# Second attention of a two-block transformer: ScalarE's order in odd works, earlier loads and values' copy, four projection chunks among the last works

## What is computed

```python
def swa_sink_mixer(h, w_in, w_out, sinks, cos, sin):      # 16 query heads, 2 key/value heads, head size 64
    q, k, v = jnp.split(h @ w_in, [qd, qd + kd], axis=-1)
    q, k = apply_rope(q), apply_rope(k)
    o = banded_attention(q, k, v, 128, sinks)             # causal, window 128
    return o @ w_out

# banded_attention, for each block of 128 queries and its 256 keys
s = q @ k.T * scale, masked to -inf outside the window
m = max(max(s), sink); e = exp(s - m)
p = e / (sum(e) + exp(sink - m));  o = p @ v
```

## Time and profile before

| | us |
|---|---|
| median of three runs (lowest, highest) | 2071.42 (2065.5, 2071.64) |
| profiled execution, its own time | 2069.99 |
| its span in the trace | 2068.2 |
| TensorE (PE) busy, share of the span | 1969.9 (95%) |
| DVE, POOL, ACT busy | 1114.8, 943.0, 695.6 |
| main part of the second attention, from `score(2)` to the output projection | 844.9 to 915.75 |

### The profile page before, as it was taken

How to read it: one execution, slowest core, us unless ns; L and a number is a source line. 1 busy time by engine, 2 the same in 40 slices (tenths; PEclk the granted TensorE clock), 3 DMA queues, 4 the chain that set the end, 5 groups by cost and what they waited for, 6 DMA issues and landing times.

```text
span 2068.2 us, 26747 instructions
## 1 busy us (share of the span) xinstructions
PE 1969.9 (95%) x10152; PEld 1616.7 (78%) x10152; DVE 1114.8 (54%) x1729; ACT 695.6 (34%) x1217; POOL 943.0 (46%) x552
## 2 busy tenths in 40 slices
PE   6999999999999999788999999999999999999997
PEld 5888776788888877667888888788897778888886
DVE  7576776864554667656422313676463338345163
ACT  3353564432222233544322213342343333222122
POOL 1465554465444445444444444543363335444442
PEclk9999999999999999999999999999999999999999
DMA  7775332455556415522333222222242123223231
GB/s 286 239 217 163 108 98 81 164 183 183 190 176 203 154 52 177 150 71 72 101 94 96 97 93 101 72 68 76 100 137 90 62 71 109 95 93 101 92 102 61
DMA packets 79986, 252.18 MB, mean 122 GB/s; under 512 B 12160, under 2 KB 12672, under 8 KB 79616
## 3 DMA queue, kind: packets, MB, share of 16 engines
q1 hardware_dynamic: 79872, 250.61, 37.3%
HBM read 235.21 MB, written 15.37 MB: 121 GB/s over the span
## 4 chain that ended last, share of the span: by engine, by line
PE 71%; issue 12%; POOL 7%; DVE 6%; ACT 3%; DMA 1%; SPq 0%; POOLq 0%; DVEq 0%; ACTq 0%
PE ps L901 19%; PE ps L903 19%; PE ps L902 19%; POOL wl L793 5%; PE ps L1150 2%; PE ps L1090 2%; PE ps L1122 2%; ACT pr L2556 1%; PE ps L1416 1%; DVE st L1859 1%; POOL al L849 1%; PE ps L1441 1%; PE ps L969 1%; POOL x L841 1%; PE ps L964 1%
## 5 line engine op out<-in xcount | busy, mean ns | idle before, releaser
L793 POOL TENSOR_TENSOR wl<-raw,wh 128x1024 fp32r<-128x1024 f32 x309 | 770.2, 2498 | 966.8 <-ACT wh L2411 966.7
L2411 ACT CAST wh<-raw 128x1024 fp32r<-128x1024 f32 x309 | 322.3, 1050 | 931.3 <-PE ps L903 854.7
L901 PE MATMUL ps<-ah,wh 128*128 128x512 f32 x1240 | 488.6, 394 | 1.5 <-DVE pair L1791 1.5
L902 PE MATMUL ps<-ah,wl 128*128 128x512 f32 x1240 | 483.4, 390 | 0.0
L903 PE MATMUL ps<-al,wh 128*128 128x512 f32 x1240 | 483.3, 390 | 0.0
L901 PEld LDWEIGHTS ps<-ah,wh 128*128 128x128 f32 x1240 | 233.2, 188 | 53.2 <-issue 3.0
L901 PE MATMUL ps<-hh,wh 128*128 128x512 f32 x688 | 271.0, 394 | 1.8 <-DVE hl L2368 1.7
L902 PEld LDWEIGHTS ps<-ah,wl 128*128 128x128 f32 x1240 | 233.3, 188 | 49.3 <-issue 1.5
L903 PEld LDWEIGHTS ps<-al,wh 128*128 128x128 f32 x1240 | 233.2, 188 | 49.2
L903 PE MATMUL ps<-hl,wh 128*128 128x512 f32 x688 | 269.9, 392 | 0.0
L902 PE MATMUL ps<-hh,wl 128*128 128x512 f32 x688 | 268.1, 390 | 0.0
(11 more groups left out here) (373 smaller groups left out, 2806.8 us busy)
## 6 DMA issues: line engine op xcount, KB each, us to landing
raw<-in_units SPq DMA_DIRECT2D x309, 512.0 KB, 3.5
ada_mlp<-in_ada SPq DMA_DIRECT2D x64, 512.0 KB, 3.4
ada<-in_ada SPq DMA_DIRECT2D x16, 512.0 KB, 16.0
qs<-qscr SPq DMA_DIRECT2D x32, 256.0 KB, 3.7
ada_in<-in_ada SPq DMA_DIRECT2D x16, 512.0 KB, 3.6
ks<-kscr SPq DMA_DIRECT2D x24, 256.0 KB, 4.6
x<-in_xT SPq DMA_DIRECT2D x1, 2048.0 KB, 13.1
qscr<-rot_h SPq DMA_DIRECT2D x16, 128.0 KB, 2.4
```

The source lines that it names most:

```text
L793: nc.gpsimd.tensor_tensor(wl[:, slot], raw[:, slot], wh[:, slot].bitcast(F32), ALU.subtract).then_inc(lo_done, 1)
L901: nc.tensor.matmul(out_ap, wh[:, slot, k], high[:, k0 + k], start=first and k == 0, stop=False)
L902: nc.tensor.matmul(out_ap, wl[:, slot, k], high[:, k0 + k], start=False, stop=False)
L2411: a.copy(wh[:, slot], raw[:, slot]).then_inc(hi_done, 1)
```

## The change

The diff has seven parts. On SP, the keys and the first two queries of group 1 are loaded ahead of the store of rotary result 10, behind two waits (result 8 stored, works 0 and 1 scored). On POOL, the last two low parts ahead of the attention wait until all 11 rotary results are made. On PE, one more unit runs ahead of the early scores (5 and 2 instead of 4 and 3 units around them). On DVE, the copy of v out of its bank (line 2124) runs between the last rotary's sums and its low part instead of behind that low part; the early attention stays behind the third query pair. On ACT, `copy(t-2)` runs ahead of `exponentials(t)` in odd steps. On PE, the first four chunks of the first unit of `swa_out` (12 matmuls) run in steps 17 and 18, two chunks ahead of `turn(15)` and two ahead of the last value; the first waits until the last work's exponentials have read the bank. `gemm_squared` then runs that unit's chunks 4 to 7 and the other seven units.

```diff
--- before.py
+++ after.py
@@ -641,10 +641,10 @@
                     sp.dma_start(qscr[4 * grp + j, 64 * low_part:64 * low_part + 64].rearrange("(a r) t -> r a t", a=2),
                                  rot[32 * j:32 * j + 32].bitcast(F32)).then_inc(rot_kept[index % 2], 16)
 
-        def loads_during(plan):
+        def loads_during(plan, first=0):
 
             for w, (g, kind, j) in enumerate(plan.works):
-                if g + 1 < GROUPS:
+                if w >= first and g + 1 < GROUPS:
                     sp.wait_ge(sc_made, plan.scored[w][-1])
                     if not plan.nsa:
                         if j == 0:
@@ -773,8 +773,13 @@
         store_q(8, 1)
         units(u + 14, u + 15)
         store_q(9, 2)
+        sp.wait_ge(rot_kept[0], rot_count(8))
+        sp.wait_ge(sc_made, PLAN_SWA.scored[EARLY - 1][-1])
+        load_k(PLAN_SWA, 1, 0)
+        for j in range(EARLY):
+            load_q(PLAN_SWA, 1, j)
         store_q(10, 3)
-        loads_during(PLAN_SWA)
+        loads_during(PLAN_SWA, EARLY)
         units(FIRST["swa_out"] + RING, FIRST["mix_out"] + 6)
         sp.wait_ge(pooled, 4)
         sp.dma_start(me[:], src["memT"]).then_inc(x_in, 16)
@@ -871,6 +876,7 @@
         added_norm(1, "swa_in")
         over_units(pool, FIRST["swa_in"] + RING, FIRST["swa_in"] + RING + 9, low)
         attention(PLAN_SWA, early=True)
+        pool.wait_ge(rot_made, 11)
         over_units(pool, FIRST["swa_in"] + RING + 9, FIRST["swa_out"] + RING, low)
         attention(PLAN_SWA)
         over_units(pool, FIRST["swa_out"] + RING, FIRST["mlp1"] + RING, low)
@@ -1009,10 +1015,26 @@
             for c in range(DC):
                 square_sum(c)
 
-        def gemm_squared(first, high, low, ready=None, ks=DC, adds=False, between=None):
-
-
-            for c in range(DC):
+        def chunks(u, k0, k1, high, low, ready):
+
+            n, slot = done[0], u % RING
+            if k0 == 0:
+                bank_free(n)
+                pe.wait_ge(lo_done, u + 1)
+            for k in range(k0, k1):
+                pe.wait_ge(ready[0], ready[1] + k + 1)
+                nc.tensor.matmul(ps[:, n % RING], wh[:, slot, k], high[:, k], start=k == 0, stop=False)
+                nc.tensor.matmul(ps[:, n % RING], wl[:, slot, k], high[:, k], start=False, stop=False)
+                mm = nc.tensor.matmul(ps[:, n % RING], wh[:, slot, k], low[:, k], start=False, stop=k == DC - 1)
+            if k1 == DC:
+                mm.then_inc(unit_used, 1)
+                done[0] += 1
+
+        def gemm_squared(first, high, low, ready=None, ks=DC, adds=False, between=None, made=0):
+
+            if made:
+                chunks(first, made, DC, high, low, ready)
+            for c in range(1 if made else 0, DC):
                 gemm(first + c, 1, high, low, ready=ready, ks=ks)
                 if between:
                     between(c)
@@ -1044,7 +1066,7 @@
                                       small("ones")[:, 0:1], start=True, stop=True)
             mm.then_inc(ada_sum, 1)
 
-        def attention(plan, early=None):
+        def attention(plan, early=None, fill=None):
 
             if not early:
                 pe.wait_ge(evac, done[0] if plan.nsa else done[0] - 1)
@@ -1158,6 +1180,11 @@
                     score(w)
                 return
             for t in range(0 if plan.nsa else EARLY, len(works) + LAG + 1):
+                if t == len(works) + 1 and fill:
+                    pe.wait_ge(p_made, plan.expd[-1][-2])
+                    fill(0, 2)
+                if t == len(works) + 2 and fill:
+                    fill(2, 4)
                 if t == EARLY + 1 and not plan.nsa:
                     pe.wait_ge(v_placed, 1)
                 if t < len(works):
@@ -1297,12 +1324,12 @@
         gemm_first(FIRST["swa_in"], ah, al, "swa_in")
         gemm(FIRST["swa_in"] + 3, 1, ah, al)
         ada_turn(7)
-        gemm(FIRST["swa_in"] + 4, 4, ah, al)
+        gemm(FIRST["swa_in"] + 4, 5, ah, al)
         attention(PLAN_SWA, early=True)
-        gemm(FIRST["swa_in"] + 8, UNITS_SWA_IN - 8, ah, al)
+        gemm(FIRST["swa_in"] + 9, UNITS_SWA_IN - 9, ah, al)
         assert done[0] % RING == 3
-        attention(PLAN_SWA)
-        gemm_squared(FIRST["swa_out"], ah, al, ready=(o_split, 2 * GROUPS), adds=True)
+        attention(PLAN_SWA, fill=lambda k0, k1: chunks(FIRST["swa_out"], k0, k1, ah, al, (o_split, 2 * GROUPS)))
+        gemm_squared(FIRST["swa_out"], ah, al, ready=(o_split, 2 * GROUPS), adds=True, made=4)
         mlp("mlp1", 32)
 
         u = FIRST["mix_in"]
@@ -1776,7 +1803,7 @@
 
         rots = [0]
 
-        def rotary(to, whole=False, query=False):
+        def rotary(to, whole=False, query=False, between=None):
 
             n = banks[0]
             a, b = ps[:, n % RING], ps[:, (n + 1) % RING]
@@ -1794,6 +1821,8 @@
             v.tensor_tensor(to[:, 2], to[:, 2], to[:, 3], ALU.add).then_inc(kc_made if whole else rot_sum, 1)
             if whole:
                 return
+            if between:
+                between()
             rotary_low(to, query)
 
         def rotary_low(to, query):
@@ -2117,11 +2146,10 @@
         rotary(pair_s)
         ada_take(7)
         ada_coef(1, 5)
-        for p in range(4):
+        for p in range(3):
             rotary(pair_s, query=True)
-            if p == 2:
-                attention(PLAN_SWA, early=True)
-        v.tensor_copy(v_t[:], bank()).then_inc(evac, 1)
+        attention(PLAN_SWA, early=True)
+        rotary(pair_s, query=True, between=lambda: v.tensor_copy(v_t[:], bank()).then_inc(evac, 1))
         attention(PLAN_SWA)
         copy_out(coef_at(1, 2))
         norm_shared("mlp1", coef_at(1, 3), coef_at(1, 4), factor=coef_at(1, 2))
@@ -2584,9 +2612,12 @@
                     exponentials(w)
                 return
             for t in range(0 if plan.nsa else EARLY, len(works) + LAG + 2):
+                copy_first = not plan.nsa and t % 2 == 1
+                if copy_first and t < len(works) + LAG:
+                    copy(t - LAG)
                 if t < len(works):
                     exponentials(t)
-                if LAG <= t < len(works) + LAG:
+                if not copy_first and LAG <= t < len(works) + LAG:
                     copy(t - LAG)
                 for unit in plan.after.get(t - LAG - 1, ()):
                     if plan.is_last(unit):
```

## The result

| | before | after |
|---|---|---|
| median of four runs each, us | 2070.68 | 2052.52 (2051.55 to 2054.64) |
| profiled execution, its own time | 2069.99 | 2054.64 |
| its span | 2068.2 | 2052.8 |

The ratio of the runs is 0.9919, interval 0.9900 to 0.9937: 0.8% faster. The medians differ by 18.2 us; the forecast had said 17.75 less than the profiled execution, 2052.2. Single runs of one kernel on one chip spread over 1.5 to 9 us, and what a part is worth is read more sharply inside the attention, between two instructions of one trace. Even there the stretches up to `score(5)` can differ by 3.3 us between two executions of the same instructions, as the last run shows.

The account below looks back on a forecast made before the run. PE, busy for 95% of the span, was taken to bound the kernel. -2.05 - 5.0 - 6.7 - 4.0 = -17.75 against the profiled 2069.99 gave 2052.2 us, range 2047 to 2061.

Parts of the forecast that it names:

- Part 1: Unit ahead of the early scores: group 0's queries land under it, PE reaches `score(2)` sooner by that wait, -2.05 us.
- Part 2: `score(2)` to `score(3)`: v copied earlier, low part without POOL's tensor_tensors, but POOL's lock moves to line 1867; 0 us.
- Part 3: `score(3)` to `score(5)`: group 1's loads moved ahead, 12.73 us becomes 7.7; -5.0 us.
- a rival had with 0.25 and 1.7 us: PE's new stop before `score(3)` is followed once by 1.2 GHz, costing up to 1.7 us: 2053.9; chance 0.25.
- the forecast's own case: Whole kernel: the parts sum to -17.75 us, 2052.2; chance 0.42.
- Part 4: Steady pairs: ACT's copy ahead in odd steps, 7.81 us a pair becomes 6.55, bound by ACT and DVE; -6.7 us.
- the rival in which it holds them back: Odd steps on ACT: the copy ahead delays the exponentials, pairs stay at 7.81, 2058.9; chance 0.07.
- Part 5: `score(15)` to the projection: waits on ACT's and DVE's copies and lost clock shrink, chunks fill the time; -4.0 us.
- The slower rival: Attention: the clock stays at 1.2 GHz throughout, a pair takes 12.6 us instead of 7.81, 2092; chance 0.02.

Follow-up runs that it names:

- the last run: Only ACT's order of the change (copies ahead of the exponentials in odd steps), on the kernel before; 2062.44 us, ratio 0.9967.
- the three further edits together: On the changed kernel: POOL's tensor_tensors behind the works, the last low part behind the values' copy, ACT's high part ahead of odd exponentials; 2049.06 us, ratio 0.9905.

## Why the prediction held, point by point

*Part 1* was right: the unit covers the queries' landing. It gave 0.27 us more than the wait in brackets; the trace of the copies alone (42.73 with a wait of 1.42) says the same, so a stop cost PE some 0.25 us beyond what its row shows.

*Part 2* came out at its price, 0, and with the mechanism named, the lock on line 1867. One sub-step was wrong: it said that POOL is released by the new wait at 845.3. POOL was still in the scales of works 0 and 1; its tensor_tensor began behind them at 846.58, which is 845.59 on the axis of before, and without the wait nothing changes. That the scales ended so near the forecast release, and the lock with them (847.95 on that axis, forecast 848.2), was luck. Nor is it the wait that frees the low part here: it runs beside the scales instead of the tensor_tensors, as in every trace with the unit ahead of the early scores, and in that of the copies alone; in the run without the unit the wait did hold POOL. The price 0 is luck in part, too: before, the low part's 3.08 us came from the same kind of meeting, which the trace of the copies alone shows missed by the same instructions, with 4.46 us for this stretch. Against that trace parts 1 to 3 give 2.76 us, not 6.03. Of the change's seven parts, POOL's wait and v's copy are worth nothing in the changed kernel, each undone by itself.

*Part 3* was mis-sized, -3.69 for -5.0. The stop of 3.25 us brought the half clock that a rival had with 0.25 and 1.7 us: the stretch takes 9.04 us against 7.37 in the kernel with the tensor_tensors late, which has the full clock there, 1.67 less, and against 7.79 in the run without the chunks, where the half clock was shorter by half. So on the trace the rival came true, and the forecast's own case, with no half clock, did not; that the median lies at 2052.5 and not at the rival's 2053.9 is within what single runs spread. That the median came within 0.3 us of the forecast is luck: the parts, in the traces, miss its sum by 1.5.

*Part 4* was right in its mechanism and 0.1 us off per pair. The loop of ACT and DVE is 6.65, not 6.55: line 1896 now falls on a multiplication of POOL's in every odd step from 5 on (0.48 for 0.23, so 0.25 more up to ACT's start), while DVE's factor and maxima took 0.13 less than their terms in the sum (0.29 and 1.36, counted from start to start, for 0.38 and 1.40). PE's own pair was put too high, at 6.32 for 6.15 or less, since the pair less its wait keeps what a stop costs beyond its row, as in part 1; the first pair ran at PE's pace, as said. The loop's rows in after, DVE's, POOL's, then ACT's:

```profile
872.79 0.16 DVE L1915 TENSOR_TENSOR st<-st 128x4 f32<-128x4 f32 x1 [0.82 <-ACT st L2587]
...
873.08 1.25 DVE L1888 TENSOR_REDUCE st<-ps 128x1 f32<-128x256 f32 x4
...
874.44 0.48 DVE L1896 TENSOR_SCALAR st<-st,neg_sinks 128x4 f32<-128x4 f32 x1
```

```profile
873.26 2.06 POOL L819 TENSOR_SCALAR pr<-pr,st,sm 128x256 f32<-128x256 f32 x4 [0.33 <-DVE st L1916]
```

```profile
873.82 0.48 ACT L2603 COPY pt<-ps 128x384 f32<-128x384 f32 x1 [0.70 <-PE ps L1144]
...
875.01 0.48 ACT L2584 ACTIVATE pr<-ps,st 128x256 f32<-128x256 f32 x1 [0.71 <-DVE st L1896]
...
876.90 0.59 ACT L2608 CAST ah<-ps 128x512 fp32r<-128x512 f32 x1
877.37 0.51 ACT L2584 ACTIVATE pr<-ps,st 128x256 f32<-128x256 f32 x1
```

The copy is done at 874.3, 0.7 us before the odd exponentials are released, so the rival in which it holds them back is out. That the loop binds was shown by the run that took its `high` out of it.

*Part 5* was right: -3.82. The chunks give 2.38 of it. The copies exchange the wait of 2.8 for waits on POOL and DVE, and what they give by themselves is the clock: 1.44 where it holds (13.06 before, 11.62 without the chunks), 0.02 where it fell again (13.04, the copies alone). Undoing the copies costs the end 2.87, and that trace has the half clock there, too.

The slower rival did not come: at 96% busy the steady part kept the full clock.

## What to carry to other kernels

When a wait on PE's path is taken away, work out the loop that binds next; here the place of one copy on ScalarE decided 1.2 us of every 7.8. A wait or a move that a trace seems to ask for may be void once another part of the same change has shifted the neighbours: undo each by itself. A collision between two engines that one trace shows may be missing from the next execution of the same instructions: before a part is priced by it, look at a second trace. And work that has time, such as GpSimd's tensor_tensors here, was better placed behind the dense chain of small VectorE operations than beside it: moving two of them gave 3.3 us more in the trace, and the three further edits together 5.2 (92.72 against 97.91; 2049.06 against 2053.55 by the medians of the same chip).

## What the runs showed of the hardware that was not expected

- A 128 x 4 tensor_scalar on DVE, 0.23 us by itself, took 1.88 beside a GpSimd tensor_tensor on 128 x 1024 (2.36 in the run with v's copy undone), to the end of it, and 0.48 beside one of GpSimd's 128 x 256 multiplications. So in these runs a tiny operation stood for 1.65 us, about as long as the low part of 128 x 1024 in the trace before (3.08 for 1.23). The Trainium skill (SBUF — State Buffer, Who interferes with whom) says that tensor_scalar can take the port pair that is shared with GpSimd, and that whichever of the two issues first has the pair for its whole instruction while the other is blocked; the runs agree.
- Of the stops of PE in this stage, those of 0.43, 1.49, 1.60, 2.05, 2.27 and 2.38 us were followed by full clock in these traces; those of 2.48 (the run without the unit) and 2.83 to 4.3 were followed by 1.2 GHz, for 3.4 or 6.8 us. A long stop isn't needed for it: in the run with the copies alone the clock fell for 3.4 us at 903.4, behind waits of 0.74, 0.42 and 0.99 that stand close together. Nor do such waits bring it each time: the run without the chunks had the same ones and kept the full clock. What decides was not settled.
- The half clock behind the same stop of 3.25 us lasted 6.8 us in five traces and 3.4 in the run without the chunks; `score(3)` to `score(5)` took 9.0 (10.88 with the loads undone) and 7.79.
